# Paired inverse roots, longer planned times for short VectorE steps up to the FFN's end, and a smaller delay ahead of turned and spread rows

## The reference

```
def rms_norm(x, g):
    xf = x.astype(jnp.float32)
    xf = xf * lax.rsqrt(jnp.mean(xf * xf, axis=-1, keepdims=True) + EPS)
    return (xf * g.astype(jnp.float32)).astype(x.dtype)
...
        h = rms_norm(x, norm1_g[l])
        z = h @ w_in[l].astype(h.dtype)
        glu_in, q, k, v, gate_logits = jnp.split(z, SPLITS, axis=-1)
        a = a_val * jax.nn.sigmoid(a_gate)
        a = causal_depthwise_conv(a, conv_w[l], conv_b[l])
        a = jax.nn.silu(rms_norm(a, conv_norm_g[l]))
        y_a = a @ w_conv_out[l].astype(a.dtype)
        q = rms_norm(q.reshape(B, S, N_HEADS, HEAD_DIM), q_norm_g[l]).astype(jnp.float32) * HEAD_DIM ** -0.5
        k = rms_norm(k.reshape(B, S, N_HEADS, HEAD_DIM), k_norm_g[l]).astype(jnp.float32)
        # attention over three dilated windows, 16 heads of 64
...
        x = x + (g_a * y_a + g_b * y_b) @ w_out[l].astype(x.dtype)
        h = rms_norm(x, norm2_g[l])
        u = causal_depthwise_conv(h @ w_up[l].astype(h.dtype), ffn_conv_w[l], ffn_conv_b[l])
        x = x + (jax.nn.silu(u_gate) * u_val) @ w_down[l].astype(x.dtype)
```

## Time and profile before

| | |
|---|---|
| median of 3 runs | 1545.22 us (1542.5, 1545.22, 1551.04) |
| profiled execution, its own time | 1542.46 us |
| its span, first to last instruction | 1540.5 us |
| busy: TensorE, VectorE, ScalarE, GpSimd | 1515.3, 1152.0, 887.0, 768.8 us |
| share of the chain that ended last: TensorE, VectorE, ScalarE | 84%, 7%, 5% |
| granted TensorE clock, mean | 0.998 |

### The profile page before, as it was taken

The page is one execution under the profiler, slowest core; times in us unless marked ns, Lnnn a source line. Parts: engine busy times, 40 slices in busy tenths (PEclk is TensorE's granted clock), DMA queues, the critical chain, the costliest instruction groups (busy, mean ns, idle before and its releaser), DMA issues.

```text
span 1540.5 us, 21821 instructions
## 1 busy us (share of the span) xinstructions
PE 1515.3 (98%) x7792; PEld 1293.6 (84%) x7792; DVE 1152.0 (75%) x2064; ACT 887.0 (58%) x1544; POOL 768.8 (50%) x726
## 2 busy tenths in 40 slices
PE   9999999999999999999999999999999999999997
PEld 7888899988888888888888888887888988888877
DVE  5999999998664687437717559967777828988977
ACT  6445788787433344324324464689995327777753
POOL 2232345435465477557747563456655424444443
PEclk9999999999999999999999999999999999999999
DMA  7889765665332222323222278856457945456551
GB/s 222 194 186 203 165 137 130 146 161 126 123 107 91 91 96 96 110 83 110 96 96 89 96 180 188 177 130 140 110 126 177 202 106 132 109 123 137 109 121 59
DMA packets 60299, 203.26 MB, mean 132 GB/s; under 512 B 6816, under 2 KB 9376, under 8 KB 60192
## 3 DMA queue, kind: packets, MB, share of 16 engines
q0 software_dynamic: 19008, 69.21, 26.3%
q1 hardware_dynamic: 40896, 132.14, 25.8%
q10 hardware_dynamic: 288, 0.52, 0.1%
HBM read 199.75 MB, written 2.10 MB: 131 GB/s over the span
## 4 chain that ended last, share of the span: by engine, by line
PE 84%; DVE 7%; ACT 5%; DMA 2%; issue 1%; POOL 1%; DVEq 0%; SPq 0%; POOLq 0%; ACTq 0%
PE bank L368 82%; PE bank L374 2%; DVE r L407 1%; DMA w_raw<-in_weights 1%; ACT k_both L378 1%; ACT prob L378 1%; ACT w_hi L378 1%; DVE pt_lo L395 1%; DMA w_lo<-in_weights 1%; DVE prob L1288 0%; ACT pt_hi L378 0%; DVE r L395 0%; DVE q_both L407 0%; DVE score L1875 0%; ACT soft L378 0%
## 5 line engine op out<-in xcount | busy, mean ns | idle before, releaser
L414 POOL TENSOR_TENSOR w_lo<-w_raw,w_hi 128x512 fp32r<-128x512 f32 (+1 forms) x190 | 278.5, 1485 | 210.3 <-ACT w_hi L378 210.3
L378 ACT ACTIVATE w_hi<-w_raw 128x1024 fp32r<-128x1024 f32 (+2 forms) x206 | 213.9, 1041 | 278.7 <-PE bank L368 253.3
L368 PE MATMUL bank<-x_hi,w_hi 128*128 128x512 f32 x872 | 346.6, 398 | 1.3 <-DVE k_lo_first L407 0.6
L368 PE MATMUL bank<-x_hi,w_lo 128*128 128x512 f32 x872 | 340.6, 391 | 0.6 <-DMA w_lo<-in_weights 0.4
L368 PE MATMUL bank<-x_lo,w_hi 128*128 128x512 f32 x872 | 340.1, 390 | 0.0
L368 PEld LDWEIGHTS bank<-x_hi,w_lo 128*128 128x128 f32 x872 | 163.7, 188 | 37.0 <-POOL w_lo L414 0.8
L368 PEld LDWEIGHTS bank<-x_hi,w_hi 128*128 128x128 f32 x872 | 163.9, 188 | 33.4 <-ACT k_both L378 1.0
L368 PEld LDWEIGHTS bank<-x_lo,w_hi 128*128 128x128 f32 x872 | 164.2, 188 | 29.8
L621 POOL DMA_DIRECT2D w_lo<-in_weights x132 | 117.0, 894 | 120.4 <-ACT w_lo L378 96.3
L368 PE MATMUL bank<-a_hi,w_hi 128*128 128x512 f32 x416 | 162.0, 389 | 0.0
L368 PE MATMUL bank<-a_hi,w_lo 128*128 128x512 f32 x416 | 161.8, 389 | 0.0
(11 more groups left out here) (230 smaller groups left out, 3403.5 us busy)
## 6 DMA issues: line engine op xcount, KB each, us to landing
w_raw<-in_weights SPq DMA_DIRECT2D x223, 512.0 KB, 3.4
w_lo<-in_weights POOLq DMA_DIRECT2D x132, 512.0 KB, 6.6
alibi<-in_alibi SPq DMA_DIRECT2D x16, 256.0 KB, 3.9
w_raw<-in_weights SPq DMA_DIRECT2D x8, 384.0 KB, 3.0
r<-in_x SPq DMA_DIRECT2D x8, 256.0 KB, 6.1
r<-in_x SPq DMA_DIRECT2D x4, 512.0 KB, 6.2
out_y<-r SPq DMA_DIRECT2D x16, 128.0 KB, 1.8
w_raw<-in_weights ACTq DMA_DIRECT2D x2, 256.0 KB, 4.2
```

Source lines behind the costliest of these rows:

```text
L368: return e.matmul(out, lhsT, rhs, start=start, stop=stop, skip_group_check=resumed)
L378: return self.act.run(lambda e: e.activation(out, in_, func, **kw), after, 0.07 + size(out) * 0.00086 + 0.09 * len(kw))
L414: return self.pool.run(lambda e: e.tensor_tensor(out, a, b, op), after, cost)
```

## The change

- `rsqrt_paired` replaces `rsqrt` in `rms` and `head_rows`. It keeps g (near the root of m) beside y (near the inverse root) in one tile `gy` and multiplies both by the same factor in one step of double width. The chain from the mean to the inverse root has 8 steps in place of 10. The layer norms of the second block keep theirs.
- In `v_tt`, `v_ts` and `v_stt` the planned cost is at least `SHORT`, 0.18 us, until `sparse_mixer` begins, and as before from there.
- `LATER` is 0.5 in place of 1.5.

```
+SHORT = 0.18
-LATER = 1.5
+LATER = 0.5
...
     def v_tt(self, out, a, b, op, after=()):
-        cost = 0.07 + size(out) * 0.00106
+        cost = max(self.short, 0.07 + size(out) * 0.00106)
...
     def v_ts(self, out, a, s1, s2, op0, op1=None, after=()):
-        cost = 0.07 + size(out) * 0.0008
+        cost = max(self.short, 0.07 + size(out) * 0.0008)
...
     def v_stt(self, out, a, s, b, op0, op1, after=()):
-        cost = 0.07 + size(out) * 0.00115
+        cost = max(self.short, 0.07 + size(out) * 0.00115)
...
+    def rsqrt_paired(self, m, gy, t, ready):
+
+        g, y = gy[:, 0, :], gy[:, 1, :]
+        tok = self.v_ts(y.bitcast(I32), m.bitcast(I32), -0.5, MAGIC, ALU.mult, ALU.add, [ready])
+        tok = self.v_tt(g, m, y, ALU.mult, [tok])
+        both = t.rearrange("p (o n) -> p o n", o=1).to_broadcast([P, 2, t.shape[-1]])
+        for n in range(3):
+            tok = self.v_stt(t, g, -0.5, y, ALU.mult, ALU.mult, [tok])
+            if n < 2:
+                tok = self.v_stt(gy, both, 1.5, gy, ALU.add, ALU.mult, [tok])
+            else:
+                tok = self.v_stt(y, t, 1.5, y, ALU.add, ALU.mult, [tok])
+        return tok
...
-        tok = self.rsqrt(m, y, t, tok)
+        tok = self.rsqrt_paired(m, gy, t, tok)
...
-        tok = self.rsqrt(mean, y, w, tok)
+        tok = self.rsqrt_paired(mean, self.pair_gy, w, tok)
...
     def sparse_mixer(self):
+        self.short = 0.0
```

More of the change, by code:

```diff
@@ L351, in __init__ @@
         self.n_streams = 0
+        self.short = SHORT
         self.beside = None
@@ L858, in spread, with rms @@
         return tok
-    def rms(self, acc, ready, eps, y):
+    def rms(self, acc, ready, eps, gy):
         yield ready
@@ L868, in rms @@
         b.release([tok])
-        tok = self.rsqrt(m, y, t, tok)
+        tok = self.rsqrt_paired(m, gy, t, tok)
+        y = gy[:, 1, :]
         yield [tok]
@@ L931, in constants @@
         self.ones = self.cols(1)
-        self.stat_m, self.stat_y, self.stat_t = self.cols(4), self.cols(4), self.cols(4)
+        self.stat_m, self.stat_t = self.cols(4), self.cols(4)
+        self.stat_gy = self.cols(8).rearrange("p (a n) -> p a n", a=2)
+        self.stat_y = self.stat_gy[:, 1, :]
         self.stat_u, self.stat_w = self.cols(4), self.cols(4)
-        self.h_inv, self.h_inv2 = self.cols(4), self.cols(4)
+        self.h_gy = self.cols(8).rearrange("p (a n) -> p a n", a=2)
+        self.h_inv, self.h_inv2 = self.h_gy[:, 1, :], self.cols(4)
         self.half_gate_b = self.cols(2 * KT)
         self.neg_q_g = self.cols(1)
-        self.pair_m, self.pair_y, self.pair_t = self.cols(16), self.cols(16), self.cols(16)
+        self.pair_m, self.pair_t = self.cols(16), self.cols(16)
+        self.pair_gy = self.cols(32).rearrange("p (a n) -> p a n", a=2)
+        self.pair_y = self.pair_gy[:, 1, :]
         self.row_min = [self.cols(NT) for _ in range(2)]
@@ L1053, in norm @@
             tok = yield from self.know(sums, KT - 1)
-            b, t, t_inv = yield from self.rms(acc[:, :], [tok, self.ones_ready, self.ident_in], 1e-6, self.h_inv)
+            b, t, t_inv = yield from self.rms(acc[:, :], [tok, self.ones_ready, self.ident_in], 1e-6, self.h_gy)
             self.wide_inv = self.ext[1]
@@ L1611, in conv_norm @@
                 yield from self.pad_known(c)
-            bank, bt, _ = yield from self.rms(self.ext[2][:, :], [self.conv_sq], 1e-6, self.stat_y)
+            bank, bt, _ = yield from self.rms(self.ext[2][:, :], [self.conv_sq], 1e-6, self.stat_gy)
             yield [bt]
@@ L1683, in norm @@
             tok = yield from self.know(self.sq_tok, KT - 1)
-            b, t, _ = yield from self.rms(self.ext[2][:, :], [tok], 1e-6, self.stat_y)
+            b, t, _ = yield from self.rms(self.ext[2][:, :], [tok], 1e-6, self.stat_gy)
             yield [t]
```

## The result

| | before | after |
|---|---|---|
| median of the runs, us | 1544.28 (6 runs) | 1548.91 (6 runs) |
| ratio of the runs, 95% interval | | 1.0036 [1.0023, 1.0049] |
| profiled execution, its own time / span, us | 1542.46 / 1540.5 | 1548.54 / 1546.6 |
| mean granted TensorE clock | 0.998 | 0.996 |

By the ratio the change makes the kernel slower by 0.36%; the two medians alone give 0.30%. That is within the 0.5% that the forecast called no change, but on the other side of it, and the median is 0.9 us above the range.

A forecast was written before the change was run, and what follows sets the result against it. TensorE was taken as the bound, resting mostly in the heads for a full VectorE. Heads -4.2, second spread +0.3 and hand-over +2.5 gave -1.4 us: 1541.1 profiled, 1542 named as the median, range 1536.5 to 1548.

The forecast's parts named there:

- the hand-over: From the heads to `attn_out`: TensorE waits longer for `w_lo1`, both halves now GpSimd's; +2.5 us, bounds 0 and +3.8.
- the split of q: Heads of the first attention: TensorE's wait of 0.5 us for this step goes, -0.5 us.
- the row minimum: Heads: its wait of 0.8 us and `pt_lo`'s of 0.4 go with fewer taps ahead, together -1.2 us.
- the first k scores: Heads: TensorE's wait of 1.3 us shrinks by 0.7 through turns 3 matmuls earlier; 0.6 stays.
- the probabilities: Heads: a wait of 1.6 us behind GpSimd's four scalings beside taps; -1.2 us taken, -1.6 at best.
- the taps are fewer by more than the wait in every one of these places: Heads: reason for taking -1.2 us on the probabilities' wait, with 3 to 8 fewer VectorE taps ahead.
- rival of stalls that only move: Heads: the new order meets as many waits as the old, so no change; 1545.3 us at most, chance 0.22.
- The second spread: Second spreading of normed rows, already waiting 0.16 us: 0.7 earlier with a chain 0.4 shorter, so +0.3 us.
- the queues from there on are the same: From the sparse attention on: argument against a further gain there, since the engines' queues keep their order.
- Its own sign of being wrong: As many waits as before in 150 to 390 us, or TensorE's idle time elsewhere changed by over 1 us.
- GpSimd as the bound of the hand-over: Hand-over to `attn_out`: ten GpSimd steps, each held by a tap, end at 399.1; 1549.5 us, chance 0.07.
- the sparse gain: Sparse attention, 1000 to 1200 us: its 5.3 idle us go, and the heads' 5.65; 1531.5 us, chance 0.05.

The follow-up runs named there:

- e12: Changed kernel with `LATER` back at 1.5, so the shorter chain and `SHORT` 0.18 only; ratio to the kernel before 1.0065.
- e16: Changed kernel with `LATER` 0.6 in place of 0.5; ratio to the kernel before 1.0030.
- e8: Kernel before with `SHORT` 0.18 alone, old chain and `LATER` 1.5; 1546.75 us, ratio to the kernel before 1.0016.
- e13: Changed kernel with `SHORT` 0.17 in place of 0.18; ratio to the kernel before 1.0068.
- e2: Changed kernel with GpSimd making both halves of `w_lo1` in a row, ahead of the first half of `w_lo2`; 1545.85 us, ratio to the kernel before 1.0019.
- e3: Changed kernel with the index scores' products back in their old places, but for two; 1548.26 us, ratio to the kernel before 1.0032.
- e5: Changed kernel with the sparse attention values' fourth block in bank 0 in place of bank 2; 1545.63 us, ratio to the kernel before 1.0010.
- e10: Kernel before with `LATER` 0.5 alone; ratio to the kernel before 1.0072.
- e14: Changed kernel with `SHORT` 0.19 in place of 0.18; ratio to the kernel before 1.0053.
- e4: Changed kernel with both halves of `w_lo1` on VectorE and the index scores' products in old places but for two; 1542.01 us, ratio to before 0.9995.
- e15: Changed kernel with `SHORT` 0.22 in place of 0.18; ratio to the kernel before 1.0004.
- e9: Kernel before with the shorter chain alone, `LATER` 1.5 and no least cost for short steps; ratio to the kernel before 1.0030.
- e11: Kernel before with the shorter chain and `LATER` 0.5, no least cost for short steps; ratio to the kernel before 1.0013.
- e7: Changed kernel with 16 overwritten matmuls added ahead of `attn_out`'s second tile; 1546.16 us, ratio to the kernel before 1.0011.

## Why the prediction was wrong

**The heads: size right, reason only half.** I forecast -4.2 us up to the hand-over and it is -3.8; the rest in 150 to 385 went from 5.2 to 1.7. Of the waits named, the split of q and the row minimum are gone but for 0.3; the first k scores kept 0.6, as forecast; the probabilities kept 0.4, as forecast; one `pt_lo` wait of 0.45 came back where I had none. The chain takes 11 steps in 2.36 us, 0.38 shorter for the 0.40 that I worked out. But the reason, "the taps are fewer by more than the wait in every one of these places", does not carry it: e12 and e16 have nearly the same sum of taps and rest 7.8 and 1.9 us. That just this order is one of the good ones was in part luck. My rival of stalls that only move, at 0.22, is what happened in all six of e8 to e13, and was underrated.

**The second spread** waits 0.45 for 0.16, +0.3 as forecast.

**What is late next: the failing step.** The sum was -1.4 us, and the profiled executions differ by +6.1. I put +2.5 on the hand-over and it was +5.3, 3.7 of wait and 1.6 of clock, and I put nothing on the index scores, where it was +3.2. The place, the engine and the kind of wait were right, and so was adding the delay to the gain: ScalarE's high part came 3.8 us earlier with TensorE and GpSimd's steps 3.3, and five kernels with quite different leads wait 3.8 to 4.5 us. That the matmul started at 392.51, where it had started at 392.56, is a coincidence of a lead of 3.8 and a delay of 3.7. The delay was priced 1.2 us too low, in three parts. Each of the three steps took 1.58 us beside the taps, not 1.41: 0.5. TensorE started 0.5 after the last one ended, for which I had nothing. And GpSimd began 1.3 us ahead of TensorE's arrival, where it had begun 1.8 ahead, held by its `x_lo`: 0.5 for the 0.3 that I took. Larger still, the clock was left out altogether, though a wait of over 2 us in an engine that never rests had one example in the trace, `out_b`'s; what the clock does behind such a wait has no place in the prediction, and behind that one it had stayed up.

**"Against it: the queues from there on are the same."** They were the same but for the banks. The prediction speaks of the order of the queues alone, not of the banks in it; the swap of banks 0 and 2 is in no step of it, and the "small stretch of the index scores" that had moved was its mark. The stretch cost 3.2 us in the profiled execution: 1.1 of wait for the swapped bank, 1.6 for a weight transfer whose cause is open, and 0.5 of shifts. The forecast had 0 there, and even gave a chance of 0.05 to a gain. Its own sign of being wrong, idle time of TensorE elsewhere changed by more than 1 us, came true: 0.4 to 2.85 us in 420 to 1000.

**The rivals.** The slower one, GpSimd as the bound of the hand-over, had 0.07 and 1549.5 us. It gave the right place, the right engine and nearly the right time, but the time by luck: its condition, ten steps each held by a tap, did not come true, and it had neither the clock nor the index scores. By the Trainium skill, page SBUF — State Buffer, section Who interferes with whom, a VectorE step with two SBUF inputs and a GpSimd step that reads SBUF lock one another out for a whole instruction. The trace agrees that they hold each other up: three taps beside `w_lo` took 1.75 to 1.80 us where a free one takes 0.74, and GpSimd's `w_lo` steps averaged 1.48 us there and 1.41 before. So the slow-down fell mostly on VectorE, and GpSimd lost some 0.1 to 0.2 us a step; whether the lock lasts a whole instruction no run here shows. The prediction's tap of 1.54 us, as long as the row scaling beside it, is no proof of it, as the two overlapped for 1.0 us only. What made the wait was that GpSimd had both halves to make (2.2 us of wait in e2) with a half of `w_lo2` between them (1.7 more). The sum of the sparse gain, 1531.5, also left out the +0.3 and +2.5 that would have stayed.

**The range** left out the sum that came true. Its upper end had no gain in the heads, +0.3 and +3.8 at the hand-over, and some 1.4 for the runs' scatter. It held nothing for the clock, 1.6, and nothing for what a new plan does after the place that it was made for, 3.2.

## What to carry to other kernels

When a new wait is added to a gain, ask first whether the late input moves with the engine that gains: here it did, since GpSimd's steps hung on what TensorE had done, and the wait was the same at any lead. Then ask what the standstill does to the clock. In a kernel whose order is made by a list scheduler, a change of costs reorders and renames far from where it acts. Read the new order with its buffer and bank numbers, and time some neighbours of a constant before believing in its mechanism: 0.17, 0.18, 0.19 and 0.22 gave 1.0068, 1.0036, 1.0053 and 1.0004. The cheapest repairs were local, made where the trace showed the new wait: both halves of one chunk on the other engine, and one bank.

## What the runs showed of the hardware

- TensorE's clock fell from 1.00 to 0.50 in or right behind standstills of 2.2 to 4.5 us in each of the eight profiles with such a wait at the hand-over (after, e2, e3, e5, e10, e13, e14, e16). That cost 1.6 to 1.7 us on top of the wait where it fell after TensorE had started again (after, e2, e10), and 2.5 to 2.8 where it was down already. Behind 1.2 us (e8, e4) it stayed at 1.00.
- The length of the standstill alone does not decide. Of the waits elsewhere, the clock fell behind 2.01 us (e15), 2.02 (e10), 2.09 (e8) and 3.10 (e9) near 1005 to 1014 us, behind 2.03 near 168 us (e11) and 3.27 near 492 us (e12), but not behind 2.38 at 197 us (e12), 2.85 at 298 us (e13) nor 2.09 at 921 us (e5). Behind one and the same standstill of 2.45 us at `out_b` it fell in 15 of 18 profiles, so two profiled executions of such kernels can differ by 1.4 us by this alone.
- 16 matmuls of no use, in a standstill of 3.9 us, kept the clock up and made the kernel faster by 1.5 us of span (e7).
- VectorE's taps took 1.75 to 1.80 us beside GpSimd's `w_lo` steps and 0.74 free of them; GpSimd's steps took 1.58 in a row beside taps and 1.41 on average before.
